# Down transfers of the expert loops issued by ScalarE instead of SyncE

## The reference

```
s = sigmoid(t @ router_w); top 6 of 64 experts, group-limited; gates normalised, x 2.5
for each expert:  hid = silu(t @ wg) * (t @ wu);  acc += (hid @ wd) * gate[:, None]
shared = (silu(t @ sh_gate) * (t @ sh_up)) @ sh_down
```

## Time and profile before

| | |
|---|---|
| median of 3 runs | 1358.21 us (1357.56 to 1358.25) |
| the profiled execution, whole | 1358.36 us |
| its span in the trace | 1356.6 us |
| TensorE matmul busy | 1299.2 us, 96% |
| VectorE / ScalarE / GpSimd busy | 481.6 / 324.2 / 78.0 us |
| moved by DMA | 447.29 MB, mean 330 GB/s |
| on q1 (SyncE's queue) | 439.25 MB, 80.0% of the 16 engines' span |
| on q10 (ScalarE's queue) | 1.01 MB |

### The profile page before, as it was taken

One profiled execution on the slowest core, in us unless ns is written; L12 is line 12 of the kernel. 1 busy time (PEld: TensorE's weight loads), 2 busy tenths in 40 slices (PEclk: granted clock), 3 DMA queues, 4 the chain that ended last, 5 costly groups with the idle time before them and its releaser, 6 DMA issues.

```text
span 1356.6 us, 17873 instructions
## 1 busy us (share of the span) xinstructions
PE 1299.2 (96%) x6452; PEld 707.9 (52%) x6452; DVE 481.6 (36%) x1079; ACT 324.2 (24%) x789; POOL 78.0 (6%) x100
## 2 busy tenths in 40 slices
PE   6988999999999999999799999999999999999995
PEld 3665744454444444544488857445544444445442
DVE  2385633333222333332422326333332223333324
ACT  1653212212121222221123222122121222221211
POOL 1333100000000000000140000000000000000000
PEclk9989999999999999999899999999999999999998
DMA  9334469999999999999861234599999999999991
GB/s 331 124 124 155 171 219 415 417 419 415 419 412 416 417 418 419 417 416 417 281 204 63 85 133 186 216 415 420 417 418 417 413 417 416 416 420 416 418 416 59
DMA packets 80323, 447.29 MB, mean 330 GB/s; under 512 B 7437, under 2 KB 25289, under 8 KB 30616
## 3 DMA queue, kind: packets, MB, share of 16 engines
q1 hardware_dynamic: 77264, 439.25, 80.0%
q0 software_dynamic: 1904, 6.46, 1.3%
q10 hardware_dynamic: 1112, 1.01, 0.2%
HBM read 445.61 MB, written 1.05 MB: 329 GB/s over the span
## 4 chain that ended last, share of the span: by engine, by line
PE 93%; issue 2%; DVE 2%; DMA 1%; ACT 1%; DVEq 0%; POOL 0%; POOLq 0%; SPq 0%
PE bank L925 33%; PE bank L947 17%; PE bank L899 10%; PE bank L993 9%; PE bank L785 4%; PE bank L749 4%; PE bank L853 2%; PE bank L662 2%; PE bank L788 2%; PE bank L935 2%; DMA ring<-in_l_w_in 1%; PE bank L962 1%; PE bank L891 1%; PE bank L644 1%; PE bank L628 1%
## 5 line engine op out<-in xcount | busy, mean ns | idle before, releaser
L925 PE MATMUL bank<-ring,big 128*64 128x512 f32 x2048 | 446.5, 594 | 0.1
L925 PEld LDWEIGHTS bank<-ring,big 128*64 128x64 f32 x2048 | 146.1, 137 | 277.9 <-issue 277.9
L947 PE MATMUL bank<-ring,big 128*64 128x512 f32 x1024 | 233.8, 598 | 2.2 <-ACT big L1205 2.2
L1601 DVE SCALAR_TENSOR_TENSOR ys_low<-bank,gcol,ys_high 128x512 fp32r<-128x512 f32 x128 | 96.1, 751 | 204.1 <-ACT ys_high L1211 204.1
L1593 DVE TENSOR_TENSOR big<-big,bank 128x256 f32<-128x256 f32 x64 | 27.0, 421 | 373.7 <-ACT big L1201 373.7
L899 PE MATMUL bank<-pick,xs_high 128*128 128x256 f32 x512 | 136.3, 301 | 0.0
L1211 ACT ACTIVATE ys_high<-bank,gcol 128x512 fp32r<-128x512 f32 x128 | 88.1, 688 | 192.1 <-PE bank L947 192.1
L947 PEld LDWEIGHTS bank<-ring,big 128*64 128x64 f32 x1024 | 67.8, 136 | 120.6 <-issue 109.6
L899 PE MATMUL bank<-pick,xs_low 128*128 128x256 f32 x512 | 126.4, 282 | 0.0
L1201 ACT ACTIVATE big<-bank 128x256 f32<-128x256 f32 x64 | 24.5, 383 | 405.7 <-PE bank L925 405.7
L899 PEld LDWEIGHTS bank<-pick,xs_high 128*128 128x128 f32 x512 | 97.6, 191 | 26.0 <-issue 24.8
(11 more groups left out here) (236 smaller groups left out, 1069.1 us busy)
## 6 DMA issues: line engine op xcount, KB each, us to landing
ring<-in_l_exp_w_gate SPq DMA_DIRECT2D x128, 1024.0 KB, 9.3
ring<-in_l_exp_w_up SPq DMA_DIRECT2D x128, 1024.0 KB, 11.4
ring<-in_l_exp_w_down SPq DMA_DIRECT2D x128, 1024.0 KB, 14.5
ring<-in_l_w_in SPq DMA_DIRECT2D x16, 1024.0 KB, 12.4
ring<-in_l_w_out SPq DMA_DIRECT2D x8, 1024.0 KB, 9.0
par<-in_l_ln_g POOLq DMA_DIRECT2D x4, 512.0 KB, 8.9
par<-in_l_ln_b POOLq DMA_DIRECT2D x4, 512.0 KB, 11.5
ring<-in_l_sh_w_gate SPq DMA_DIRECT2D x2, 1024.0 KB, 6.6
```

Source lines behind the costliest of these rows:

```text
L925: ins = mm(ps[SLOTS * q:SLOTS * q + SLOTS, :], xg[:, c, SLOTS * j:SLOTS * j + SLOTS], both[:, c], start=(c == 0), stop=(c == C - 1))
L947: ins = mm(ps[SLOTS * q:SLOTS * q + SLOTS, :], hidT[pr][:, m, SLOTS * q:SLOTS * q + SLOTS], wt[:, m, HALF * h:HALF * h + HALF], start=(m = ...
L1601: ins = v.scalar_tensor_tensor(ys[1][:, pr, part], ps[:], gcol[:, pr:pr + 1], ys[0][:, pr, part], ALU.mult, ALU.subtract)
```

## The change

The helper `expert_weights`, which gives the source of an expert's weights, moves from `prog_sync` to where all engines' programs can call it. In SyncE's first loop only the first `2 * GE` entries of `IN_ORDER` are left, the gate and up transfers. ScalarE's `rows(pr)`, behind its second scaling of the pair, issues the two down transfers of that pair for the next group. They need no wait of their own: the second scaling has waited for the second down bank of the pair, which is what SyncE waited for. The second loop (`more`) keeps all of its transfers on SyncE (`lp.r is None` excludes it). Transfers per group, their sizes, buffers and semaphores are the same.

```diff
@@ prog_sync, first loop
                 with sp.Fori(1, NGRP) as i:
                     lp.i = i
-                    for j, w in IN_ORDER:
+                    for j, w in IN_ORDER[:2 * GE]:
 
                         _, full, _, n = lp.at(last_use_of_weights(j, w), back=1)
                         sp.wait_ge(full, n + 1)
@@ prog_scalar, group
                             ps = lp.read(act, ("dn", pr, h))
                             fn(ys[0][:, pr, HALF * h:HALF * h + HALF], ps[:], ACT.Copy, scale=gcol[:, pr:pr + 1])\
                                 .then_inc(lp.sem("high"), 1)
+                        if lp.r is None and not last:
+                            for j in (2 * pr, 2 * pr + 1):
+                                act.dma_start(loop_weights(L, j, 2), expert_weights(L, lp.groups(GE, GE + j), 2))\
+                                   .then_inc(S(f"unit_full{loop_unit(L, j, 2)[0]}"), 16)
```

More of the change, by code:

```diff
@@ L470, in loop_weights, with expert_weights @@
             return by_chunk(a) if w < 2 else by_pair(a)
+        def expert_weights(L, e, w):
+            src = I[f"l{L}_exp_w_{('gate', 'up', 'down')[w]}"][bass.ds(e, 1)]
+            return src.rearrange("a (p c) f -> (a p) c f", c=C) if w < 2 else \
+                src.rearrange("a (p m) n -> (a p) m n", m=2)
         def prog_sync(sp):
@@ L478, in load @@
                 sp.dma_start(dst, src).then_inc(S(f"unit_full{units.at[key][0]}"), 16)
[L480 to L483, removed]
             for tb in range(TB):
```

## The result

The changed kernel takes 1381.22 us (median of 4 runs, 1376.82 to 1382.42) against 1358.23; the ratio is 1.0157, with a 95% interval of 1.0139 to 1.0176. (The ratio is taken over all runs and not from the two medians, whose quotient is 1.0169.) By the medians it is slower by 23 us where 17 were forecast, and inside the range of 1361 to 1391.

The account below looks back on a forecast made before the run. TensorE's own work was taken as the bound. A copy delay of 0.15 us and a transfer stall of 0.41 us made 0.56 us a group, 17 us over 30 groups, so 1358.4 + 17 = 1375 us, range 1361 to 1391.

Parts of the forecast that it names:

- TensorE is the bound, transfers have 6.8 us of room: Expert loops: TensorE's work sets the 30.19 us group; pair 1's gate and up land 6.8 us before needed.
- SyncE's removed waits: SyncE's loop: four waits and four issues fewer a group, claimed worth 0.
- The hold: ScalarE's issues delay its pair 1 flipped-rows copy, making down late by 0.15 us a group, bounds 0 and 0.75.
- the row at 8.06: Kernel start: ScalarE issued a transfer while its activation from 8.05 ran 0.60 us more; taken as sign of early issue.
- held longer: Rival, ScalarE before pair 1's copy: issues start later or take twice 0.81 us; 1381 to 1391 us, chance 0.17.
- The second pair's issues hidden: ScalarE, pair 1's down issues before two gather copies: what these feed starts 5 us later, cost 0.
- Halves by packet: Two DMA queues with work take turns by packet; packets being alike, gate and up go at half speed.
- The stall for transfers: Start of pair 1's gate and up: TensorE waits 0.41 us a group for the last up transfer, slowed by sharing.
- The two stalls replace each other: Group period: a larger stall at down of pair 1 shrinks that at gate and up; growth 0.53 to 0.75 us.
- Order kept: Rival, DMA queues: what is queued first is mostly served first, only the copy delay left; 1363 us, chance 0.14.
- Lower rate: Rival, DMA: two streams lower the rate to 369 GB/s against 417, 51 us more, 1409 us; chance 0.06.
- not slower: Other side: ScalarE held under 0.25 us and gate and up keep over 60% of bandwidth; 1358 us, no change 0.08.

Follow-up runs that it names:

- 4: Changed kernel, but only pair 1's down transfers issued by ScalarE, pair 0's back on SyncE behind gate and up; 1361.4 us, ratio 1.0004 to the kernel before.
- 1: Changed kernel, but all four down issues moved behind ScalarE's last gather copy of the group; 1360.9 us, ratio 1.0008 to the kernel before.
- 8: Changed kernel with pair 0's down issues behind ScalarE's copy for pair 1, and down weights in 4 KiB packets; 1354.3 us, ratio 0.9954 to before.
- 7: Kernel before the change, all transfers on SyncE, with down weights in 4 KiB packets and flip columns to match; 1354.6 us, ratio 0.9964 to before.
- Experiment 6: Changed kernel with down weights in packets of 4 KiB instead of 8 and flip columns to match; 1369.8 us, ratio 1.0065 to the kernel before.
- 5: Kernel before, all weights on SyncE, plus small unread ScalarE transfers, one per expert, at the change's place; 1367.3 us, ratio 1.0053 to before.

## Why the prediction was right, and where not

- **TensorE is the bound, transfers have 6.8 us of room.** Right, 6.0 to 7.2 us over the groups of the trace before. 4 spends part of that room and costs nothing.
- **SyncE's removed waits are worth 0.** Right: all four are gone in 1 and 8 and two in 4, and nothing is gained (in 8, nothing beyond 7).
- **The hold** was right in place and kind and too small: 0.15 us a group taken, 0.27 measured, 8.2 us and not 4.5. The issues do not begin with the scaling, as I took from the row at 8.06, but 0.14 to 0.25 us behind it, and a pair lasts 0.85 us and not 0.81. The early start is there, with a hold of 0.05 us, only in the groups written out behind the loop, which have no register instructions for the address. The rival "held longer" had named that address; I put it down with the rival and charged nothing for it. Of the two bounds, 0 and 0.75, the lower was the nearer, as chosen. This term is most of the 6 us between 1375 and 1381.
- **The second pair's issues hidden.** Right (4).
- **Halves by packet.** Right, 292 to 292. The Trainium skill has the rule ("DMA: Bandwidth & Descriptors", Queues, rings and completion order): each DMA engine goes round the queues that have work, one packet from each. Experiment 6 agrees, 260 packets to 257 with packets of unequal size, where what the profile counts as a packet is one piece of 8 or 4 KiB. The statement that the prediction weighed, of the Trainium skill ("Trainium Kernel Development and Optimization", Key Constraints), that issuing from several engines only saves issue time, fits the rate, 426 GB/s shared and 417 before. It does not hold for the time of this kernel: the order of landing changed, and with it the time.
- **The stall for transfers** was right in sum, 12 us forecast and 11.9 and 14.8 measured, and wrong in form. I took 0.41 us in every group, and it came in 7 and 9 groups of 30, by up to 3.3 us. My sum let the first gate transfer land at 5.7 us because the queue is not yet empty. It lands then because the last engine of 16 is late; the median one is at 4.8, and a lone transfer's is at 4.5. The typical last up transfer landed after 20.8 us and not after some 22. By these records there would be no stall without a late engine, so the sum came out by luck. "The two stalls replace each other" was not shown either: without the hold, 7.4 us were left and not more.
- **The rest.** The first down transfer landed 9.1 us after its issue (median) and not after some 7; nothing hung on it. 2 to 3 us of the 23 lie outside the loops and were in no term.
- **The rivals.** "Order kept" falls by the landings, 18.3 us at the least where it was 14.8. "Held longer" had the right cause for a part and the wrong size: the copy started 1.03 us behind the scaling and not 1.57, and 5 has the hold alone at 7.3 us. "Lower rate" falls by 426 GB/s in the shared window; "not slower" failed at both its points, the copy at 1.03 us and the half share.

## What to carry to other kernels

Taking a stream of transfers to another queue changes which transfer lands when, even if nothing is issued earlier: find the transfers that are wanted first and ask whether the moved ones can now run beside them. On a compute engine each issue stands in that engine's order, so put it behind whatever another engine is waiting for; here the two issues of pair 0 cost 8 us behind the scaling and nothing one instruction later. Count room to the landing of the latest DMA engine, over many groups and not one: here it was up to 1.8 us behind the median engine with one queue and up to 4.4 us with two.

## What was not expected of the hardware

A transpose on TensorE of 128 x 128 float32 that reads adjacent columns was 0.035 us shorter than one that reads every second column (0.37 us for two against 0.44). The smaller packets cost no bandwidth that showed: 417 GB/s in the loops before (195 to 646 us), 417 in the same window of experiment 7, and 418 in the mixed window of experiment 6. An issue's price on ScalarE depended on where its address came from: 0.83 us a pair, started with the scaling, where the address was fixed in the program, and 0.85 us a pair, started 0.14 to 0.25 us later, where registers gave it.
